# Two of a layer's weight halves are loaded and split during the row gathers instead of behind them

## The reference, cut to what matters

```python
    # end of the first block, for each block of 128 tokens
    u = expert_down[eidx]                                    # (128, 8, 16, 1024), gathered rows
    a = jax.nn.gelu(jnp.einsum('thkd,td->thk', u, xb), approximate=False)
    coef = g * a
    y = jnp.einsum('thk,thkd->td', coef, expert_up[eidx])    # the second half of the same rows
    h = h + y
    x = rmsnorm(h, g_final)
    # start of the second block
    h = rms_norm(x, norm_mix)
    u = h @ w_in                                             # gq, gk, gv, ... are slices of u
```

## Time and profile before

| | |
|---|---|
| median of 3 runs | 1416.81 us (1415.72 to 1417.44) |
| the profiled execution's own time | 1418.8 us |
| its span in the profile | 1417.1 us |
| TensorE busy | 1264.8 us (89%) |
| VectorE busy | 949.0 us (67%) |
| ScalarE busy | 586.1 us (41%) |
| GpSimd busy | 276.6 us (20%) |
| gathered rows | 256 DMAs, 268.45 MB |
| weight halves | 118 DMAs of 1024 KB |

### The profile page before, as it was taken

One profiled execution on the slowest core, in us unless ns is written; L12 is line 12 of the kernel. 1 busy time (PEld: TensorE's weight loads), 2 busy tenths in 40 slices (PEclk: granted clock), 3 DMA queues, 4 the chain that ended last, 5 costly groups with the idle time before them and its releaser, 6 DMA issues.

```text
span 1417.1 us, 15243 instructions
## 1 busy us (share of the span) xinstructions
PE 1264.8 (89%) x5458; PEld 866.5 (61%) x5458; DVE 949.0 (67%) x1979; ACT 586.1 (41%) x1045; POOL 276.6 (20%) x281
## 2 busy tenths in 40 slices
PE   7999998988787888888787777799999999999998
PEld 6887896634343333434343222488688788888887
DVE  5756566877777777777777776655756556777445
ACT  5646453432223232222322223465456644555344
POOL 1000000443533434343433433000000000000000
PEclk9999999799899999989999999999999999999999
DMA  7433533999999999999999999745354345455551
GB/s 282 179 119 104 179 119 105 419 420 421 422 421 422 421 421 415 422 411 421 421 422 421 422 421 421 296 163 178 117 183 161 134 174 182 181 182 201 186 203 61
DMA packets 57122, 398.71 MB, mean 281 GB/s; under 512 B 7112, under 2 KB 7624, under 8 KB 9176
## 3 DMA queue, kind: packets, MB, share of 16 engines
q0 software_dynamic: 36864, 268.45, 45.7%
q1 hardware_dynamic: 18000, 125.84, 24.7%
q10 hardware_dynamic: 2184, 3.45, 0.7%
HBM read 396.67 MB, written 1.05 MB: 281 GB/s over the span
## 4 chain that ended last, share of the span: by engine, by line
PE 55%; DMA 26%; DVE 8%; ACT 7%; issue 3%; ACTq 0%; POOL 0%; SPq 0%; DVEq 0%
PE ps L799 34%; DMA B<-in_ex,eidx 25%; PE ps L1135 10%; PE ps L827 4%; DVE B L2458 3%; ACT hl L1411 2%; PE ps L828 2%; DVE hl L1980 1%; DMA ring<-in_wt 1%; ACT diags L1678 1%; ACT L1671 1%; ACT L1667 1%; ACT av_ L1671 1%; PE ps L1044 0%; PE ps L1026 0%
## 5 line engine op out<-in xcount | busy, mean ns | idle before, releaser
L1135 PE MATMUL ps<-B,diags 128*128 128x512 f32 x1024 | 487.7, 623 | 119.2 <-ACT diags L1678 118.1
L1135 PEld LDWEIGHTS ps<-B,diags 128*128 128x128 f32 x1024 | 191.5, 196 | 388.7 <-issue 198.4
L2458 DVE CUSTOM_DVE_ANT_0 B<-B 128x1024 f32<-128x1024 f32 x256 | 311.5, 1221 | 121.6 <-DMA B<-in_ex,eidx 121.5
L763 POOL DMA_INDIRECT B<-in_ex,eidx x256 | 270.6, 1057 | 614.2 <-PE ps L1135 361.5
L1980 DVE TENSOR_TENSOR hl<-ring,hl 128x2048 fp32r<-128x2048 f32 x116 | 265.5, 2290 | 184.3 <-ACT hl L1411 184.1
L1411 ACT ACTIVATE hl<-ring 128x2048 fp32r<-128x2048 f32 x116 | 221.6, 1912 | 117.6 <-PE ps L799 114.3
L799 PE MATMUL ps<-hl,R 128*128 128x512 f32 x960 | 223.6, 392 | 0.3 <-DVE R L1996 0.3
L799 PE MATMUL ps<-hl,XT 128*128 128x512 f32 (+1 forms) x888 | 203.4, 387 | 4.8 <-DVE hl L1980 4.4
L1671 ACT ACTIVATE av_<-av_ 128x2 f32<-128x2 f32 x128 | 26.0, 203 | 432.9 <-DVE av_ L2458 432.8
L799 PEld LDWEIGHTS ps<-hl,R 128*128 128x128 f32 x960 | 178.7, 188 | 38.0 <-DVE R L1996 0.7
L799 PEld LDWEIGHTS ps<-hl,XT 128*128 128x128 f32 x888 | 162.4, 188 | 40.6 <-DVE hl L1980 5.6
(11 more groups left out here) (356 smaller groups left out, 964.6 us busy)
## 6 DMA issues: line engine op xcount, KB each, us to landing
ring<-in_wt SPq DMA_DIRECT2D x117, 1024.0 KB, 4.8
B<-in_ex,eidx POOLq DMA_INDIRECT x256, 13.0
X<-in_x SPq DMA_DIRECT2D x2, 512.0 KB, 4.4
B<-in_mem ACTq DMA_DIRECT2D x1, 1024.0 KB, 10.8
ring<-in_wple SPq DMA_DIRECT2D x1, 1024.0 KB
out<-B SPq DMA_DIRECT2D x3, 256.0 KB, 2.0
GB<-in_gffn ACTq DMA_DIRECT2D x1, 512.0 KB, 3.6
GB<-in_gfin ACTq DMA_DIRECT2D x1, 512.0 KB, 7.1
```

Source lines behind the costliest of these rows:

```text
L763: e.indirect_dma_start(out=rows[i % NG][:, :], out_offset=None, in_=A["ex"], in_offset=bass.IndirectOffsetOnAxis(ap=eidx[:, tb, s:s + 1], ...
L1135: m = e.matmul(acc[tb][hf][:, :], diags[:, i % 4, :], rows[i % NG][:, 1024 + 512 * hf:1536 + 512 * hf], start=(s == 0), stop=(s == 127))
L2458: m = e.tensor_tensor_reduce(R[:, 0:1024], R[:, 0:1024], XG[:, tb, :], 1.0, 0.0, ALU.mult, ALU.add, av_[:, tb, s + z:s + z + 1])
```

## The change

SyncE issues the first two `gv` halves during the rows: the first when row 159 has landed, the second when row 223 has. Each is cut into two DMAs, of 120 and of 8 partitions, that count on a semaphore of their own. ScalarE and VectorE split them between pairs of the last head's first token block (h = 7, tb = 0), ScalarE behind pairs 1 and 5, VectorE behind pairs 2 and 6. The wait for row 254 now stands ahead of the third half, `("gv", 1, 0)`. The calls `split_to(n + 1)` and so on behind the rows stay in the text, and find halves n and n + 1 done.

```diff
-            ld.update(count(f"ring{i}", [n for n in range(len(HALVES)) if n % RING == i], 16))
+            ld.update(count(f"ring{i}", [n for n in range(len(HALVES)) if n % RING == i and HALVES[n][:2] != ("gv", 0)], 16))
+
+        BETWEEN = {NUM["gv", 0, 0]: 159, NUM["gv", 0, 1]: 223}
+        for n in BETWEEN:
+            ld[n] = count(f"between{n}", ["most", "rest"], 16)["rest"]
...
@@ SyncE @@
-                if n in (NUM["gv", 0, 0], NUM["gv", 0, 1]):
-                    e.wait_ge(*gath[254 + n - NUM["gv", 0, 0]])
+                if n in BETWEEN:
+                    e.wait_ge(*gath[BETWEEN[n]])
+                    for p, m in ((0, 120), (120, 8)):
+                        e.dma_start(ring[p:p + m, n % RING, :], A["wt"][FIRST[name] + 2 * k + h][p:p + m, :]).then_inc(ld[n][0], 16)
+                    continue
+                if n == NUM["gv", 1, 0]:
+                    e.wait_ge(*gath[254])
...
@@ ScalarE, in the loop over the rows @@
+                        if h == 7 and tb == 0 and n in (1, 5):
+                            split_to(NUM["gv", 0, n // 4])
...
@@ VectorE, in the loop over the rows @@
+                        if h == 7 and tb == 0 and n in (2, 6):
+                            split_to(NUM["gv", 0, n // 4])
```

## The result

| | before | after |
|---|---|---|
| median | 1417.12 us (6 runs) | 1430.91 us (6 runs, 1428.63 to 1432.82) |
| ratio, 95% interval | | 1.0096 [1.0082, 1.011] |
| the profiled execution's own time | 1418.8 us | 1428.63 us |
| its span | 1417.1 us | 1426.9 us |
| TensorE / VectorE busy | 1264.8 / 949.0 us | 1269.8 / 948.9 us |

The change makes the kernel 1.0% slower: 13.8 us by the medians, 9.8 by the two profiled executions. I forecast 3.1 slower. 1430.91 lies far above the range's end of 1421.0.

The account below looks back on a forecast made before the run. It took the rows to be bound by bytes on the DMA engines. Rows +5.3, tail -2.2 and splits at nothing gave +3.1 us, a median of 1419.9; the 8-in-10 range reached from the spared engine's 1414.6 to 1415.1 up to 1421.0.

Parts of the forecast that it names:

- Part 2: In the DMA-bound rows: the two added loads lengthen them by 5.3 us, with bounds below 0 and above 5.6.
- Part 1: Behind the last row: without the two splits there, TensorE goes on 2.2 us earlier, bounds 2.0 to 4.4.
- Part 3: Among the rows: four splits moved there cost nothing; 1.6 us for both if the queued rows gave no cover.
- The last engine is spared: Rows' end: the late DMA engine gets no packet of either piece, loads cost 0, time 1414.6 to 1415.1; chance 20%.
- The whole 4.4 us: Behind the rows: the chain to the diagonal is hidden, the tail gains 4.4 us, time 1417.7; chance 6%.
- the splits stall the rows: In the rows: gathers issued late because of the splits land late, 1.6 us on top, time 1421.5; chance 4%.
- the forecast's own case: Whole kernel: longer rows less the shorter tail, 1418.9 to 1420.7 us; chance 70%.

## Why the prediction was wrong

**The step that failed** is Part 2's bound above: "an engine that gets one of them on top of eight has 9/8 of 2.49 = 2.80 us", and with it "above 2 x 2.80 = 5.6". The 5.3 us taken for the rows measured 14.65. The base of the step was right: a whole load costs the rows 2.4 us (4.80 for two, against 4.98), and with whole loads the kernel measured 1420.38, 0.23% above the one before, where 4.98 - 2.2 is 0.20%. What the step lacked is that a packet's 0.31 us isn't a constant, neither for the load's packets (0.52) nor for the rows' beside it (0.57). The earlier trace rows priced loads that all spread over 128 partitions, and I carried their price to other shapes by counting packets per engine. The packets' number was as counted; their length doubled. Of the 14.65 us, 4.80 are bytes and 9.85 the shape of the pieces.

**What the pieces do, and how far that is shown.** Shown: in the slow stretches the DMA share stays at 1.0 and the rate falls, at the lowest to 228 GB/s for the change, 241 for 120, 264 for 112 + 16 and 246 for 64 + 64 neighbouring partitions. With 120 + 8 it does so with or without rows beside them (219). It doesn't for 128 partitions, for columns, or for even and odd partitions. Not shown: where in the chip the packets wait. No row of the profile numbers engines or ports. Not shown either is which side of the transfer counts: a piece of neighbouring partitions also reads neighbouring rows of the weights, and no run changed the one without the other.

The Trainium skill has a map that bears on it ("DMA: Bandwidth & Descriptors", section "The descriptor swizzle", and "SBUF — State Buffer", section on the DMA port swizzle): the memory has 16 ports for DMA, each for two groups of four partitions that lie 32 apart, the partitions 0 to 63 on the even ports and 64 to 127 on the odd ones, and in a transfer over 128 partitions each engine writes one port alone. By that map the partitions 0 to 63 reach 8 ports of 16, which goes with the low rate of the 64 + 64 run. The 120 partitions reach all 16; by the map they are slow only if their fifteen engines no longer have a port each and meet on the same ones, which would happen if an engine's share were neighbours, 0 to 7, 8 to 15 and so on. But then an engine of the even piece would have 0, 2, 4 and 6, the next 8 to 14, and they would meet on the same ports in the same way, and the even and odd pieces cost the rows 4.76 us against the 120's 13.35. So the map goes with 64 + 64 and by itself doesn't tell the 120 from the even and odd pieces; which engine wrote which partition no run here shows, and the cause stays open there. The 1.1 us of a load of four or eight partitions doesn't follow from it by any count of mine, and stays open.

**Part 1, the tail**, was right: 2.56 us against 2.2 with bounds 2.0 to 4.4, and in its order. TensorE does the two groups directly behind the last row, ScalarE's split (927.78 to 929.68) is what the root at 929.59 waits for, and VectorE's split stands behind the diagonal. TensorE's idle time in front of the turn is 1.9 us, not 1.5. What I did not foresee is that TensorE's clock can be low just behind this idle time. Leaving out the even and odd pieces, thirteen profiled executions have this code behind the rows and 1.9 us of idle TensorE in it. In seven, the change's among them, the turn took 2.02 us and the 36 matmuls started 15.35 or 15.36 behind the last dot product's start, 2.55 sooner than before. In the other six (without loads, whole loads, 112 + 16, 64 + 64, 120 alone, 124 to 127 alone) it took 2.79 to 3.56 us and they started 15.68 to 16.63 behind it. That takes back 0.3 to 1.3 us of the gain there, and up to 0.9 more in the 36 matmuls.

**Part 3, the splits in the rows at nothing**, was right: 0.15 us in the run without loads. There VectorE's first split makes the dot product of row 230 2.1 us late, not 0.8, and by row 234 nothing is left of it; the second makes that of row 238 1.1 us late, and by row 239 it is back.

**The rivals.** *The last engine is spared*: no. The rows did not end at 904 to 905, and one engine's long tail at the rows' end is there as before (share 0.10 at 41 GB/s behind 913, after; the earlier trace rows have 0.08 and 0.07):

```profile
911.00:913.00 2.00, 2.00 (x6) 0.92 (x5) 1.27 (x5) 1.73 (x7) 0.00 (x0) 1.00 0.76 315
913.00:915.00 2.00, 1.14 (x3) 0.19 (x1) 2.00 (x3) 0.00 (x0) 0.00 (x0) 1.00 0.10 41
```

Whether the late engine was left out of the 120 partitions can't be told from this, since the row packets were slow too, 0.57 us on average, and no row tells one engine from another. The rule of the Trainium skill on how many engines take part ("DMA: Bandwidth & Descriptors", section on why a DMA increments its semaphore by 16) agrees with the profile's packet count: q1 has 18014 packets instead of 18000, seven more for each of the two loads, 15 + 8 semaphore packets in place of 16. That number did not decide: 112 + 16 and 64 + 64, with 16 and 16 semaphore packets a load, are slow as well. *The whole 4.4 us* and *the splits stall the rows* did not come true either.

**A slip in the range.** The lower end of the forecast's own case, 1416.81 + 4.98 - 2.4 - 0.3, is 1419.1 and not 1418.9. It changes nothing in the outcome.

## What to carry to other kernels

In a stretch that is bound by DMA, a load's price is its bytes only if it is laid out over the partitions as the loads are from which the price is taken. Cut a tile by columns, not into runs of neighbouring partitions (4.9 to 5.4 against 11.1 to 14.7 us here for 2.1 MB), and look at share and GB/s together: a share of 1.0 with half the rate is packets that last longer, not more bytes. And price a load into a DMA-bound stretch against what it frees: here each whole load costs 2.4 us to win at most half of a 2.6 us tail.

## What was unexpected of the hardware

- A DMA of 0.98 MB over 120 neighbouring partitions costs a saturated stretch 6.7 us, one of 1.05 MB over 128 partitions 2.4 us; two of 64 neighbours 6.3, the even and the odd 64 2.4.
- A load of 32 KB on four partitions costs the saturated stretch 1.1 us, as much as 64 KB on the partitions 0 to 7: for 2 us the row packets beside it take 0.54 us instead of 0.31. Why is open.
- 17 partitions in one DMA, with one semaphore packet, make the rows 4.25 us late, of which 3 had been caught up 56 rows later.
- Idle time of 1.9 us on TensorE in front of the turn came with a granted clock of 0.72 just behind it in the run without loads, and 1.00 in the changed kernel with the same code there; in thirteen such executions the turn was slow in six.
